# A two-layer hybrid encoder step on one core: when GpSimd adds up layer 1's weight sums in HBM

## The chip, the core and the metric

The kernel runs on one core of a Trainium2 chip. The time is device microseconds of one execution, the median of several runs. The profile is one further execution, recorded by the hardware profiler.

## What is computed

One step of a streaming encoder with two layers over 576 tokens: 512 of a prompt and 64 of a later chunk that attends to 512 cached positions. All arithmetic is float32.

```
h = rmsnorm(x, g_pre_mix);  z = h @ w_in
y_a = b_g * causal_depthwise_conv3(c_g * xin)
y_b = multi-head latent attention (8 heads, rotary key, chunk-causal mask)
x = x + rmsnorm((sigmoid(ga) * y_a + sigmoid(gb) * y_b) @ w_o, g_post_mix)
f = square(relu(rmsnorm(x, g_pre_ffn) @ w1)) @ w2      # 1024 -> 4096 -> 1024
x = x + rmsnorm(f, g_post_ffn)
```

## The kernel before

Features lie on the partitions and tokens on the free axis, in two halves of 288 tokens. Each float32 product is made of three float32r matmuls (mm3, L811 to L813) from a high and a low part of weight and input; ACT copies the high part of a weight block (w_hi), DVE subtracts it from the raw block (w_lo, L2071). The five engines run programs written out by hand, each in order, and meet only through semaphores.

A layer goes through the latent projections (P1), eight heads, the output projection w_o with the later chunk's attention between its blocks, and the feed-forward in eight groups of 512 hidden features (GROUPS). SyncE loads the weights into nine slots as 512 KB blocks (slot_load, L859) or as halves of 256 KB.

Where both token halves are multiplied by the same two-by-two blocks of a weight, the kernel makes seven block products in place of eight, in Strassen's manner (Winograd's form). That needs sums and differences of weight quarters. There are two places:

- Heads 2 to 6 (MIXED of them, two pairs of blocks each). Their weight sums don't depend on data, and GpSimd makes them in HBM, in the tensor weight_sums, by DMAs: one copy of a block's first half into two places and two further copies (sums_copy, L1129 to L1131), then four DMAs that add to what they write (L1135, L1136, L1139, L1142). A sum is four quarters; there are N_SUMS = 20, ten a layer. sums_steps(n0, n1) issues them in a software pipeline: round n copies for sum n + 1, adds first to n, second to n - 1 and third to n - 2, each after the semaphore of what it builds on. SyncE loads finished sums from HBM (L949 and L954) behind a wait on sums_third.
- Feed-forward groups 2 to 7. There DVE makes the sums in SBUF (pair_sums, L3009 to L3014) once both blocks of a couple have landed. A couple, pair(g, p) in the code, is half of a group: seven products into the four PSUM banks named ring (r_pair(g, p, i) numbers them). After the couple come eight products with w2 into the four banks named att (w2_blocks); DVE adds them to my (w2_out, L2923), which frees the bank for the product four later.

In group 3 and later, DVE's order after a couple's last ring product is fixed: the next couple's four pair_sums, one low part of f, the first w2_out, and so on (outs_and_lo). SyncE issues the next couple's first block (pair_load(g, p, 0)) after this couple's second product and the second block after its fifth. ACT takes the first block's high part (block_hi, L1845) before the couple's second output.

GpSimd's program is short: the sums, the rotation of the key in both layers (key_rope, L1175 to L1184) and part of the last addition (L1198). It issues the first two rounds of sums before layer 0's key rotation (BEFORE_KEYS = 2) and all the others right after it, in one sequence over both layers' sums. In head 7 SyncE also loads the caches for the later chunk (L995 to L999), which ACT and DVE split (L1556, L1557, L1567) before they go on with that head's convolution and gates. The last head's merged rows (xs_hi, L1661; xs_lo, L2744) are what w_o needs first.

Of the kernel before, what the change touches and what calls it, by code (L numbers as in the profile page):

```python
# [53 lines left out]
def n_head(h, i):  # L54
    return N_P1 + N_HEAD * h + i
# [30 lines left out]
MIXED = LAST_MIXED - FIRST_MIXED + 1  # L86
# [83 lines left out]
N_SUMS = DEPTH * 2 * MIXED  # L170
BEFORE_KEYS = 2
# [26 lines left out]
def pair_no(L, g, p):  # L198
    return L * PAIRS + 2 * (g - FIRST_PAIR) + p
# [32 lines left out]
def r_pair(g, p, i):  # L232
    return R5 + 7 * pair_no(0, g, p) + i
# [103 lines left out]
def root(L, name):  # L337
    return len(ROOTS) * L + ROOTS.index(name) + 1
# [380 lines left out]
def full(L, idx):  # L719
    return L * RING + (idx + 1)  # L720
# [78 lines left out]
def cols(s):  # L799
    return slice(NH * s, NH * (s + 1))  # L800
# [313 lines left out]
def rotation_and_sums(nc, block, pl, blocks):  # L1114


    @block.gpsimd
    def _(pool):

        def first_and_second(n):  # L1120

            L, i = divmod(n, 2 * MIXED)
            row = n_head(FIRST_MIXED + i // 2, (2, 0)[i % 2])
            return blocks[L * NB + row], blocks[L * NB + row + 1]

        def sums_copy(n):
            a, b = first_and_second(n)
            a11 = a[:, 0:512].unsqueeze(1).broadcast_to([P, 2, 512])
            pool.dma_start(pl.sums[n][:, 0:2, :], a11).then_inc(pl.sums_copied, 16)  # L1129
            pool.dma_start(pl.sums[n][:, 2, :], b[:, 0:512]).then_inc(pl.sums_copied, 16)  # L1130
            pool.dma_start(pl.sums[n][:, 3, :], a[:, 512:1024]).then_inc(pl.sums_copied, 16)  # L1131

        def sums_add_first(n):
            _, b = first_and_second(n)
            pool.dma_start(pl.sums[n][:, 2, :], b[:, 512:1024], accum_op=ALU.add).then_inc(pl.sums_first, 16)  # L1135
            pool.dma_start(pl.sums[n][:, 1, :], b[:, 0:512], accum_op=ALU.add).then_inc(pl.sums_first, 16)  # L1136

        def sums_add_second(n):
            pool.dma_start(pl.sums[n][:, 0, :], pl.sums[n][:, 2, :], accum_op=ALU.add).then_inc(pl.sums_second, 16)  # L1139

        def sums_add_third(n):
            pool.dma_start(pl.sums[n][:, 3, :], pl.sums[n][:, 0, :], accum_op=ALU.add).then_inc(pl.sums_third, 16)  # L1142

        def sums_steps(n0, n1):

            for n in range(n0, n1):
                if n < N_SUMS:
                    pool.wait_ge(pl.sums_copied, 48 * (n + 1))
                if 1 <= n <= N_SUMS:
                    pool.wait_ge(pl.sums_first, 32 * n)  # L1150
                if 2 <= n <= N_SUMS + 1:
                    pool.wait_ge(pl.sums_second, 16 * (n - 1))
                if n >= 3:
                    pool.wait_ge(pl.sums_third, 16 * (n - 2))
                if n + 1 < N_SUMS:
                    sums_copy(n + 1)
                if n < N_SUMS:
                    sums_add_first(n)
                if 1 <= n <= N_SUMS:
                    sums_add_second(n - 1)  # L1160
                if n >= 2:
                    sums_add_third(n - 2)

        pool.sem_inc(pl.ring_free, 4)
        pool.sem_inc(pl.w2_free, 4)
        pool.sem_inc(pl.summed, 2)
        pool.sem_inc(pl.pv_read, 1)

        def key_rope(L, half):

            cs, n = cols(half), 2 * L + half
            pool.wait_ge(pl.key_swapped, n + 1)
            if half == 1:
                pool.wait_ge(pl.key_roped, n)
            nc.gpsimd.tensor_tensor(pl.rope1_t[:, :], pl.kpe[:, cs], pl.cos[:, cs], ALU.mult) \  # L1175
                .then_inc(pl.key_turned, 1)
            nc.gpsimd.tensor_tensor(pl.rope1_s[:, half, :], pl.rope1_s[:, half, :], pl.sin[:, cs], ALU.mult) \
                .then_inc(pl.key_turned, 1)
            pool.wait_ge(pl.key_turned, 3 * n + 2)
            nc.gpsimd.tensor_tensor(pl.rope1_t[:, :], pl.rope1_t[:, :], pl.rope1_s[:, half, :], ALU.add) \  # L1180
                .then_inc(pl.key_turned, 1)
            pool.wait_ge(pl.key_turned, 3 * n + 3)
            pool.wait_ge(pl.rooted, root(L, ("rx_a", "rx_b")[half]))
            nc.gpsimd.tensor_tensor(pl.kpe[:, cs], pl.rope1_t[:, :], pl.rx[:, cs], ALU.mult) \  # L1184
                .then_inc(pl.key_roped, 1)

        pool.wait_ge(pl.x_landed[7], 16)
        sums_copy(0)
        sums_steps(0, BEFORE_KEYS)
        for L in range(DEPTH):  # L1190
            pool.wait_ge(pl.tables_landed, L * 32 + 32)
            key_rope(L, 0)
            key_rope(L, 1)
            if L == 0:
                sums_steps(BEFORE_KEYS, N_SUMS + 2)
        for i, (m0, m1) in enumerate(TAIL_MOVED):
            pool.wait_ge(pl.tail_factored, i + 1)
            nc.gpsimd.tensor_tensor(pl.x[:, m0:m1, cols(1)], pl.x[:, m0:m1, cols(1)], pl.last[:, m0:m1, :], ALU.add) \  # L1198
                .then_inc(pl.tail_moved, 1)
# [2782 lines left out]
```

## Time and profile before

| what | value |
|---|---|
| median of 3 runs | 1727.48 us (1726.52 to 1728.12) |
| the profiled execution's own time | 1726.3 us |
| its span | 1724.5 us |
| mean granted TensorE clock | 0.997 |
| TensorE busy | 1705.7 us, 99% |
| VectorE busy | 1309.3 us, 76% |
| ScalarE busy | 855.1 us, 50% |
| GpSimd busy | 122.3 us, 7% |
| HBM read and written | 214.39 MB and 57.02 MB |

The span runs from the first to the last instruction. PE is TensorE, DVE VectorE, ACT ScalarE, POOL GpSimd and SP SyncE; a q behind a name is the engine's instruction queue. Numbers with L are lines of the kernel. Layer 1 runs the same instructions as layer 0 some 850 us later, so that a moment of one layer can be compared with the other's. The time to landing of a DMA runs from its issue to its semaphore.

### The profile page before, as it was taken

How to read it: one execution, taken by the hardware profiler on the slowest of the kernel's cores; microseconds unless marked ns; L12 is line 12 of the kernel's file. 1: busy time of each engine (PE TensorE's matmuls, PEld its weight loads, DVE VectorE, ACT ScalarE, POOL GpSimd, SP SyncE). 2: the span in 40 equal slices, each digit the busy share in tenths (PEclk: the TensorE clock that was granted, in tenths of full speed). 3: DMA queues.
4: the chain of work that ended last, by engine and by line, in shares of the span. 5: the costliest groups of instructions: out<-in, count | busy, mean ns of one | idle time of the engine just before them, and what ended most of it. 6: DMA issues, size and time to landing. Idle time of an engine off the chain costs nothing.

```text
span 1724.5 us, 31894 instructions
## 1 busy us (share of the span) xinstructions
PE 1705.7 (99%) x12735; PEld 1690.9 (98%) x12735; DVE 1309.3 (76%) x2514; ACT 855.1 (50%) x1665; POOL 122.3 (7%) x163
## 2 busy tenths in 40 slices
PE   9999999999999999999999999999999999999997
PEld 9998999999999999999999999999999999999997
DVE  7788787767798786668687797777678887777665
ACT  7625454545465454436366364545435536444452
POOL 1412121212210000000001000000000000000000
PEclk9999999999999999999999999999999999999998
DMA  7899898898762232323124454343532213322231
GB/s 239 198 212 244 214 209 211 178 249 235 163 129 97 89 96 86 99 86 111 60 84 149 148 166 139 114 121 112 171 117 98 99 37 111 98 86 87 74 99 55
DMA packets 90996, 231.54 MB, mean 134 GB/s; under 512 B 9824, under 2 KB 25440, under 8 KB 90848
## 3 DMA queue, kind: packets, MB, share of 16 engines
q1 hardware_dynamic: 71968, 185.45, 33.5%
q0 software_dynamic: 17600, 41.95, 13.8%
q8 instruction: 101, 1.65, 0.4%
q10 hardware_dynamic: 1280, 2.10, 0.3%
q14 instruction: 47, 0.39, 0.1%
HBM read 214.39 MB, written 57.02 MB: 157 GB/s over the span
## 4 chain that ended last, share of the span: by engine, by line
PE 94%; DMA 2%; DVE 2%; ACT 1%; SPq 1%; issue 0%; DVEq 0%; ACTq 0%
PE ring L811 19%; PE ring L813 19%; PE ring L812 19%; PE att L811 11%; PE att L813 11%; PE att L812 11%; PE att L3527 1%; DMA cache_pe_raw<-cache_pe_in 1%; PE att L806 1%; PE att L805 1%; DMA small_raw<-small_in 1%; DMA xs_lo_raw<-h_kept 1%; PE att L818 0%; ACT rope_s L1291 0%; PE att L3343 0%
## 5 line engine op out<-in xcount | busy, mean ns | idle before, releaser
L811 PE MATMUL ring<-xs_hi,w_lo 128*128 128x288 f32 x1872 | 556.6, 297 | 4.3 <-DVE xs_lo L2744 2.2
L813 PE MATMUL ring<-xs_hi,w_hi 128*128 128x288 f32 x1872 | 551.4, 295 | 0.0
L812 PE MATMUL ring<-xs_lo,w_hi 128*128 128x288 f32 x1872 | 551.3, 294 | 0.0
L2071 DVE TENSOR_TENSOR w_lo<-w_raw,w_hi 128x1024 fp32r<-128x1024 f32 (+1 forms) x364 | 370.0, 1035 | 37.3 <-ACT w_hi L1220 27.2
L811 PEld LDWEIGHTS ring<-xs_hi,w_lo 128*128 128x128 f32 x1872 | 351.6, 188 | 7.3 <-DVE ga L2355 2.4
L812 PEld LDWEIGHTS ring<-xs_lo,w_hi 128*128 128x128 f32 x1872 | 351.7, 188 | 1.4
L813 PEld LDWEIGHTS ring<-xs_hi,w_hi 128*128 128x128 f32 x1872 | 351.5, 188 | 0.0
L813 PE MATMUL att<-f_hi,w_hi 128*128 128x288 f32 x960 | 283.2, 295 | 0.0
L812 PE MATMUL att<-f_lo,w_hi 128*128 128x288 f32 x960 | 282.9, 295 | 0.0
L811 PE MATMUL att<-f_hi,w_lo 128*128 128x288 f32 x960 | 282.6, 294 | 0.0
L811 PEld LDWEIGHTS att<-f_hi,w_lo 128*128 128x128 f32 x960 | 180.4, 188 | 0.0
L812 PEld LDWEIGHTS att<-f_lo,w_hi 128*128 128x128 f32 x960 | 180.4, 188 | 0.0
L813 PEld LDWEIGHTS att<-f_hi,w_hi 128*128 128x128 f32 x960 | 180.4, 188 | 0.0
L1212 ACT ACTIVATE w_hi<-w_raw 128x1024 fp32r<-128x1024 f32 x98 | 101.9, 1053 | 87.0 <-DMA w_raw<-blocks_in 86.8
L1220 ACT ACTIVATE w_hi<-w_raw 128x1024 fp32r<-128x1024 f32 x118 | 122.8, 1051 | 7.2 <-DMA w_raw<-blocks_in 6.5
L2923 DVE TENSOR_TENSOR my<-att,my 128x288 f32<-128x288 f32 x160 | 70.8, 451 | 67.7 <-PE att L813 67.7
L813 PE MATMUL ring<-mix_hi,w_hi 128*128 128x288 f32 x384 | 113.5, 295 | 0.0
L811 PE MATMUL ring<-mix_hi,w_lo 128*128 128x288 f32 x384 | 113.1, 295 | 0.0
L812 PE MATMUL ring<-mix_lo,w_hi 128*128 128x288 f32 x360 | 105.9, 294 | 0.0
L811 PE MATMUL ring<-turn_hi,w_lo 128*128 128x288 f32 x320 | 94.9, 296 | 0.0
L812 PE MATMUL ring<-turn_lo,w_hi 128*128 128x288 f32 x320 | 94.4, 295 | 0.0
L813 PE MATMUL ring<-turn_hi,w_hi 128*128 128x288 f32 x320 | 94.2, 295 | 0.0
(342 smaller groups left out, 3184.4 us busy)
## 6 DMA issues: line engine op xcount, KB each, us to landing
w_raw<-blocks_in SPq DMA_DIRECT2D x195, 512.0 KB, 3.7
weight_sums<-blocks_in POOLq DMA_DIRECT2D x80, 256.0 KB, 7.2
w_raw<-blocks_in SPq DMA_DIRECT2D x62, 256.0 KB, 4.6
weight_sums<-blocks_in POOLq DMA_DIRECT2D x20, 512.0 KB, 5.6
weight_sums<-weight_sums POOLq DMA_DIRECT2D x40, 256.0 KB, 7.6
w_raw<-weight_sums SPq DMA_DIRECT2D x20, 512.0 KB, 4.6
w_raw<-weight_sums SPq DMA_DIRECT2D x40, 256.0 KB, 4.4
small_raw<-small_in SPq DMA_DIRECT2D x16, 320.0 KB, 4.6
```

The lines of the kernel that those rows point to most:

```text
L805: pe.matmul(out, both, keys[1], start=False, stop=False)
L806: return pe.matmul(out, both, keys[0], start=False, stop=True)
L811: pe.matmul(out, w[1], x[0], start=first, stop=False)
L812: pe.matmul(out, w[0], x[1], start=False, stop=False)
L813: return pe.matmul(out, w[0], x[0], start=False, stop=last)
L1212: act.activation(hi, raw, ACT.Copy).then_inc(pl.weights_hi, 1)
L1220: act.activation(hi, raw, ACT.Copy).then_inc(pl.weights_hi, 1)
L2071: return dve.tensor_tensor(out, a, hi.bitcast(F32), ALU.subtract)
L2923: dve.tensor_tensor(dst, src, dst, ALU.add).then_inc(pl.w2_free, 1)
L3527: last = pe.transpose(att[:, to:to + P], pl.probs[:, PO[t] + P * j:PO[t] + P * (j + 1)], ident)
```

## The change

sums_steps takes two further arguments, the first sum and the end of the stretch that its pipeline runs over. GpSimd now runs it over layer 0's ten sums alone, to the end (2 * MIXED = 10), waits until the last is done and until the ring product r_pair(2, 1, 0) of layer 0 is full, and then runs it over layer 1's ten. r_pair(2, 1, 0) is the first product of the second couple of feed-forward group 2. The other engines' programs are as before.

```diff
--- before.py
+++ after.py
@@ -1141,24 +1141,24 @@
         def sums_add_third(n):
             pool.dma_start(pl.sums[n][:, 3, :], pl.sums[n][:, 0, :], accum_op=ALU.add).then_inc(pl.sums_third, 16)
 
-        def sums_steps(n0, n1):
+        def sums_steps(n0, n1, first, end):
 
             for n in range(n0, n1):
-                if n < N_SUMS:
+                if n < end:
                     pool.wait_ge(pl.sums_copied, 48 * (n + 1))
-                if 1 <= n <= N_SUMS:
+                if first < n <= end:
                     pool.wait_ge(pl.sums_first, 32 * n)
-                if 2 <= n <= N_SUMS + 1:
+                if first + 1 < n <= end + 1:
                     pool.wait_ge(pl.sums_second, 16 * (n - 1))
-                if n >= 3:
+                if n > first + 2:
                     pool.wait_ge(pl.sums_third, 16 * (n - 2))
-                if n + 1 < N_SUMS:
+                if n + 1 < end:
                     sums_copy(n + 1)
-                if n < N_SUMS:
+                if n < end:
                     sums_add_first(n)
-                if 1 <= n <= N_SUMS:
+                if first < n <= end:
                     sums_add_second(n - 1)
-                if n >= 2:
+                if n > first + 1:
                     sums_add_third(n - 2)
 
         pool.sem_inc(pl.ring_free, 4)
@@ -1186,13 +1186,17 @@
 
         pool.wait_ge(pl.x_landed[7], 16)
         sums_copy(0)
-        sums_steps(0, BEFORE_KEYS)
+        sums_steps(0, BEFORE_KEYS, 0, 2 * MIXED)
         for L in range(DEPTH):
             pool.wait_ge(pl.tables_landed, L * 32 + 32)
             key_rope(L, 0)
             key_rope(L, 1)
             if L == 0:
-                sums_steps(BEFORE_KEYS, N_SUMS + 2)
+                sums_steps(BEFORE_KEYS, 2 * MIXED + 2, 0, 2 * MIXED)
+                pool.wait_ge(pl.sums_third, 16 * 2 * MIXED)
+                pool.wait_ge(pl.ring_full, full(0, r_pair(2, 1, 0)))
+                sums_copy(2 * MIXED)
+                sums_steps(2 * MIXED, N_SUMS + 2, 2 * MIXED, N_SUMS)
         for i, (m0, m1) in enumerate(TAIL_MOVED):
             pool.wait_ge(pl.tail_factored, i + 1)
             nc.gpsimd.tensor_tensor(pl.x[:, m0:m1, cols(1)], pl.x[:, m0:m1, cols(1)], pl.last[:, m0:m1, :], ALU.add) \
```

GpSimd's instructions, in order, behind layer 0's key rotation, from the round that copies for the eleventh sum (layer 1's first). Before:

```order
L1129 DMA weight_sums<-blocks_in 128x2x512 [waits sums_second,sums_third,sums_first,sums_copied]
L1130 DMA weight_sums<-blocks_in 128x512
L1131 DMA weight_sums<-blocks_in 128x512
L1135 DMA weight_sums<-blocks_in 128x512
L1136 DMA weight_sums<-blocks_in 128x512
L1139 DMA weight_sums<-weight_sums 128x512
L1142 DMA weight_sums<-weight_sums 128x512
```

The same place with the change:

```order
L1135 DMA weight_sums<-blocks_in 128x512 [waits sums_second,sums_third,sums_first,sums_copied]
L1136 DMA weight_sums<-blocks_in 128x512
L1139 DMA weight_sums<-weight_sums 128x512
L1142 DMA weight_sums<-weight_sums 128x512
L1139 DMA weight_sums<-weight_sums 128x512 [waits sums_third,sums_second,sums_first]
L1142 DMA weight_sums<-weight_sums 128x512
L1142 DMA weight_sums<-weight_sums 128x512 [waits sums_third,sums_second]
L1129 DMA weight_sums<-blocks_in 128x2x512 [waits ring_full,sums_third]
L1130 DMA weight_sums<-blocks_in 128x512
L1131 DMA weight_sums<-blocks_in 128x512
L1129 DMA weight_sums<-blocks_in 128x2x512 [waits sums_copied]
L1130 DMA weight_sums<-blocks_in 128x512
```

The round's three copies are gone from there, the pipeline drains over three rounds, and the copies for layer 1's first sum stand behind a wait on ring_full; from there the ten sums follow each other as the first ten did.

## Rows read from the trace of the kernel before

**Rows 1.** The page: TensorE's busy time, and the chain that ended last, by engine

```profile
PE 1705.7 (99%) x12735; PEld 1690.9 (98%) x12735; DVE 1309.3 (76%) x2514; ACT 855.1 (50%) x1665; POOL 122.3 (7%) x163
...
PE 94%; DMA 2%; DVE 2%; ACT 1%; SPq 1%; issue 0%; DVEq 0%; ACTq 0%
```

**Rows 2.** Timeline of PE: start, duration (us), instruction, idle time before and its releaser

```profile
136.47 0.50 PE L811 MATMUL att<-probs_t_hi,v_lo 128*128 128x512 f32 x1 [2.44 <-DVE probs_t_lo L2071]
...
402.92 0.37 PE L811 MATMUL ring<-xs_hi,w_lo 128*128 128x288 f32 x1 [2.21 <-DVE xs_lo L2744]
```

**Rows 3.** Table by stage; the first row names its columns

```profile
core 0: us, PE busy (x) PEld busy (x) DVE busy (x) ACT busy (x) POOL busy (x), PEclk, DMA share, GB/s
160.00:372.00 212.00, 212.00 (x1565) 208.77 (x1564) 165.04 (x334) 102.59 (x191) 44.38 (x60) 1.00 0.86 207
372.00:410.00 38.00, 35.79 (x267) 35.22 (x267) 27.73 (x63) 20.03 (x45) 6.88 (x9) 1.00 0.96 239
457.00:510.00 53.00, 53.00 (x402) 53.00 (x401) 51.67 (x107) 33.49 (x73) 11.01 (x14) 1.00 0.70 155
591.00:791.00 200.00, 200.00 (x1512) 200.00 (x1511) 143.03 (x266) 94.92 (x187) 0.00 (x0) 1.00 0.30 90
1008.00:1222.00 214.00, 213.65 (x1576) 210.34 (x1576) 167.00 (x336) 104.63 (x196) 0.00 (x0) 1.00 0.42 127
1222.00:1258.00 36.00, 36.00 (x270) 35.65 (x269) 27.46 (x61) 19.22 (x43) 0.00 (x0) 1.00 0.48 150
```

**Rows 4.** Issues of the sums (first and last start, us); timeline of PE, second couple

```profile
L1129 POOL DMA_DIRECT2D weight_sums<-blocks_in x20: 724/751/885, 19.2 to 458.8; - x20
...
L949 SPq DMA_DIRECT2D w_raw<-weight_sums x20: 319/323/339, 116.6 to 1183.5; - x20
...
589.14 0.29 PE L811 MATMUL ring<-xs_hi,w_lo 128*128 128x288 f32 x1
```

**Rows 5.** Timeline of SP, ACT and DVE around head 7's cache loads, in both layers

```profile
375.67 0.43 SPq L981 DMA_DIRECT2D small_raw<-small_in  x1
...
1226.57 0.43 SPq L981 DMA_DIRECT2D small_raw<-small_in  x1
...
390.78 1.06 ACT L1556 ACTIVATE cache_t_hi<-cache_t_raw 128x1024 fp32r<-128x1024 f32 x1 [1.99 <-DMA cache_pe_raw<-cache_pe_in]
...
402.32 0.45 DVE L2744 SCALAR_TENSOR_TENSOR xs_lo<-my,xs_hi 128x288 fp32r<-128x288 f32 x1
...
1250.11 0.45 DVE L2744 SCALAR_TENSOR_TENSOR xs_lo<-my,xs_hi 128x288 fp32r<-128x288 f32 x1
```

**Rows 6.** Timeline of PE and DVE at a couple's end in layer 0's feed-forward

```profile
706.78 0.29 PE L811 MATMUL att<-f_hi,w_lo 128*128 128x288 f32 x1
...
719.50 0.29 PE L811 MATMUL ring<-xs_hi,w_lo 128*128 128x288 f32 x1
...
707.40 0.69 DVE L3009 TENSOR_TENSOR w_raw<-w_raw 128x512 f32<-128x512 f32 x1
...
710.31 0.45 DVE L2923 TENSOR_TENSOR my<-att,my 128x288 f32<-128x288 f32 x1
```

**Rows 7.** DMA issues, median us to landing: 160:372 (two), 1008:1222 (two), 591:791 (one)

```profile
w_raw<-blocks_in SPq DMA_DIRECT2D x10, 512.0 KB, 7.9
w_raw<-weight_sums SPq DMA_DIRECT2D x9, 512.0 KB, 5.7
...
w_raw<-blocks_in SPq DMA_DIRECT2D x10, 512.0 KB, 3.5
w_raw<-weight_sums SPq DMA_DIRECT2D x9, 512.0 KB, 3.8
...
w_raw<-blocks_in SPq DMA_DIRECT2D x34, 512.0 KB, 3.5
```

**Rows 8.** The page's queues: packets, MB, time as a share of 16 engines' span

```profile
q1 hardware_dynamic: 71968, 185.45, 33.5%
q0 software_dynamic: 17600, 41.95, 13.8%
```

## The prediction, as made before the change was run

> **What bounds the kernel now.** The page first: TensorE is busy 1705.7 us of a span of 1724.5 us, and 94% of the chain that ended last is its own work [rows 1]. So a change pays only where TensorE stands still, and costs only where it makes TensorE stand still. TensorE's waits come next, and where they lie in time: the two longest are 2.44 us at 136.47 us, for the probabilities' low parts, and 2.21 us at 402.92 us, for xs_lo of L2744 [rows 2]. The first lies while layer 0's own sums are under way, which the change leaves as they are. The table by stage then shows that of layer 0's stages from 160 us on TensorE is idle in one alone, 372 to 410 us (35.79 of 38.00 us busy), and that the DMA engines are 0.86 busy in the heads (160 to 372 us) and 0.96 there, against 0.42 and 0.48 in the same stages of layer 1, where no sums are made; in the feed-forward they are 0.30 busy [rows 3]. The granted clock is 1.00 in every one of these rows, so it plays no part.
>
> **What the change moves.** Nothing is removed. Twenty sums are issued by GpSimd, from 19.2 us on, the last one's copy at 458.8 us [rows 4]: one per 23.1 us, and two further rounds end the last, at some 505 us. The first ten (layer 0's) keep their place. The other ten, layer 1's, now wait until the first product of group 2's second couple is full. That couple's products begin at 589.14 us [rows 4] and a product takes 1.59 us (below), so the wait ends at 590.7 us. Behind it on GpSimd stand only the sums themselves and, after them, layer 1's key rotation. SyncE waits for sums before it loads them, in layer 0 first at 116.6 us [rows 4]; layer 1 runs 850.90 us behind (below), so its first such load is due at 967.5 us. With 20 to 23 us each the ten sums end at 790 to 820 us: nobody is late for them, this costs nothing, and the cover is some 150 us. Two extra bursts on GpSimd's queue (the tail of the first ten, the start of the second ten) cost nothing either, GpSimd being idle there. What is left is the traffic: it goes out of some 300 to 505 us and comes into 591 to about 810 us.
>
> **The gain, at 402.9 us.** Head 7 loads its small block, the cache and weight blocks close together. The small block's issue on SyncE at 375.67 us has its twin in layer 1 at 1226.57 us, 850.90 us later. ACT stands idle 1.99 us for cache_pe in layer 0; at the end of the chain DVE's xs_lo starts at 402.32 us, where the twin (1250.11 less 850.90) would start at 399.21 us: 3.11 us late, of which TensorE waits 2.21 us [rows 5]. The twin makes TensorE wait for nothing. The instructions are the same; what differs is the sums' traffic. The whole 2.21 us should go. Bounds: nothing (if the load order alone made it) and 2.21 us; I take 2.2, since the twin is the nearest row there is. What is late next there has 0.9 us in hand (3.11 less 2.21).
>
> **The loss, from 591 us on.** Here the reader must look at how narrow a couple's schedule is. TensorE makes seven ring products and then eight att products; the latter begin at 706.78 us and the next couple at 719.50 us, that is 1.59 us a product, and 15 of them or 23.85 us a couple. The fifth att product starts halfway, at 713.14 us, and needs its bank emptied by DVE's first L2923, which ends at 710.31 + 0.45 = 710.76 us: 2.4 us in hand [rows 6]. In front of it on DVE, which works in order, stand the four weight sums L3009 to L3014. The first starts at 707.40 us, when the couple's second weight block lands (it lands 3.5 us after its issue, the median of all 34 loads of the stretch [rows 7]; the issue follows TensorE's fifth product at 719.50 − 23.85 + 5 × 1.59 = 703.6 us, so the two agree), and DVE works without a pause from there to L2923. So a block that lands d late makes TensorE wait d − 2.4 us, once per couple. The couple's first block holds ACT in the same way, but was issued three products earlier; I leave it out.
>
> How late does a load land beside the sums? The trace has it for the heads, with equal loads in both layers. Ten 512 KB loads from blocks_in land in 7.9 us (median) in 160 to 372 us and in 3.5 us in layer 1: d = 4.4. Nine loads from weight_sums: 5.7 against 3.8 us, d = 1.9 [rows 7]. Over the slack of 2.4 that is 2.0 us for ten and nothing for nine: 20/19 = 1.05 us a load. The feed-forward loads less itself (DMA share 0.30 against 0.42 [rows 3]), so less queues behind a late load: 1.05 × 0.30/0.42 = 0.75 us. The sums last 200 to 230 us, that is nine couples: 9 × 0.75 = **6.7 us**. Bounds: nothing, if every d stays under 2.4 (the nine), and 9 × 2.0 = 18 us if every load is as late as the median of the ten.
>
> What speaks against this loss is the size of a load in engine time. The rows on the queues [rows 8]: SyncE's queue holds 16 engines for 33.5% of 1724.5 us for 185.45 MB, so 1.63 us for a 512 KB load; GpSimd's 13.8% is 238 us, 11.9 us a sum, half of the time in which sums are made. If the engines took turns evenly, a load of 1.63 us would be held up by about as much again, 1.6 us, less than the slack; the ten loads at d = 4.4 say that it is more. The Trainium skill, DMA: Bandwidth & Descriptors, section Queues, rings and completion order, states such turns: each DMA engine goes round the queues that have work, a whole packet at a time. By that rule the loss would be nought and the change would give 2.2 us. By the rows the loss is 6.7 us, and I go by them; even turns stay a rival.
>
> **Sum.** 1726.3 us is the profiled execution's time, 1.2 us under the median of the runs (1727.48). 1726.3 − 2.2 + 6.7 = 1730.8; on the median's footing 1727.5 + 4.5 = **1732.0 us**.
>
> **Rivals.** (1) The slack holds: the sums find the DMA engines 70% idle, their turns are even, d stays under 2.4 us, and only the 2.2 us at 402.9 us remain: 1725.3 us, not slower. For it: 457 to 510 us, with sums and weight loads at once, shows no wait of TensorE (53.00 us of 53.00 busy [rows 3]). Against it: the medians of rows 7 (the loads of 457 to 510 us may have more time before their use). It decides at d = 2.4 us. (2) The sums fall into step with the couples (20 to 23 us against 23.85 us) and hit the sensitive load nearly every time: 9 × 2.0 = 18 us, 1743 us. Against it: the two cadences differ by 1 to 4 us, so over nine couples they drift through each other. (3) The couples' loads get by, and the wait at 136.47 us shrinks as well: 1727.5 − 2.2 − 2.4 = 1722.9 us. Nothing in the trace ties that wait to layer 1's sums. (4) The wait passes at once and nothing moves: excluded by the value it waits for, which the ring reaches first at 590.7 us.
>
> **Chances.** What a measurement of this kernel can tell from no change is 0.2%, 3.5 us. The forecast has 0.53: its own spread is a loss of 4 to 11 us, net +2 to +9, and a quarter of it (0.13) stays within 3.5 us. Rival 1 has 0.33, rival 2 0.08, rival 3 0.06. So slower 0.40 + 0.08 = 0.48, same 0.13 + 0.33 = 0.46, faster 0.06. The predicted time is the forecast's. The range goes down to rival 1 with a little room, 1724.5, and up to a net +11, 1738.5, short of rival 2. The forecast's own range is 1729.5 to 1736.5.
>
> **What would show it.** In the changed kernel's trace: GpSimd's copies stop near 250 us and start again at about 591 us; DMA share near 0.45 to 0.5 in 372 to 510 us and 0.7 or more in 591 to 800 us; the wait for xs_lo L2744 gone from TensorE's list; w_raw's landing time in 591 to 791 us at 5 us or more; and new TensorE waits for my of L2923, each 0.5 to 2.5 us, at the fifth att product of a couple. The forecast is wrong if those waits are missing or add up to less than 3 us, if the landing times stay under 5.9 us, or if the wait at 402.9 us stays.

## The result, and the profile after

The changed kernel takes 1730.27 us (median of 13 runs, 1726.34 to 1732.39) against 1725.07 us for the kernel before on the same chips (13 runs, 1723.38 to 1728.12). The ratio is 1.0023, with a 95% interval from 1.0014 to 1.0032: 4.0 us slower, 2.4 to 5.5 (the ratio is formed over runs side by side, so it isn't that of the two medians). Its profiled execution has a span of 1730.6 us, 6.1 us above that of before, and its own time, 1732.39 us, is the longest of the 13.

TensorE's list of waits in the changed kernel (us in total, times, longest). L2927 is L2923 of before, L2075 is L2071; the change put four lines ahead of them:

```profile
PE att L811 <- DVE my L2927: 6.3, 5, 2.5
PE att L811 <- DVE probs_t_lo L2075: 2.1, 1, 2.1
```

The wait for xs_lo of L2744, 2.21 us before [rows 2], is no longer in the list; five waits for my take its place. The wait for probs_t_lo is still there (2.1 us against 2.4). Where the five lie, from the timeline of TensorE (start, duration, idle time before it):

```profile
615.94 0.40 PE L811 MATMUL att<-xs_hi,w_lo 128*128 128x288 f32 x1 [0.63 <-DVE my L2927]
...
640.57 0.40 PE L811 MATMUL att<-xs_hi,w_lo 128*128 128x288 f32 x1 [0.50 <-DVE my L2927]
...
738.02 0.40 PE L811 MATMUL att<-f_hi,w_lo 128*128 128x288 f32 x1 [1.53 <-DVE my L2927]
...
763.27 0.40 PE L811 MATMUL att<-f_hi,w_lo 128*128 128x288 f32 x1 [1.14 <-DVE my L2927]
...
789.83 0.40 PE L811 MATMUL att<-f_hi,w_lo 128*128 128x288 f32 x1 [2.46 <-DVE my L2927]
```

The table by stage of the changed kernel, to be held against [rows 3] (the same columns):

```profile
372.00:410.00 38.00, 38.00 (x286) 37.65 (x285) 29.50 (x68) 19.91 (x46) 0.00 (x0) 1.00 0.52 174
457.00:510.00 53.00, 53.00 (x402) 53.00 (x402) 50.30 (x104) 33.51 (x75) 0.00 (x0) 1.00 0.24 80
591.00:791.00 200.00, 193.74 (x1453) 192.33 (x1452) 134.55 (x252) 93.74 (x182) 46.17 (x63) 1.00 0.82 186
```

TensorE is now fully busy at head 7 and idle 6.3 us in the feed-forward. The DMA share fell from 0.96 to 0.52 at head 7 and from 0.70 to 0.24 in 457 to 510 us, and rose from 0.30 to 0.82 in 591 to 791 us: the traffic went where the prediction put it. GpSimd's wait ended at 589.0 us and the weight loads beside the sums land in 6.0 us in place of 3.5 [rows 7], 2.5 us late:

```profile
589.00 0.75 POOL L1129 DMA_DIRECT2D weight_sums<-blocks_in  x1 [331.72 <-PE ring L813]
...
w_raw<-blocks_in SPq DMA_DIRECT2D x33, 512.0 KB, 6.0
```

The sums' last DMA landed at 817.6 us. All eight couples of the loop over groups 3 to 6 lie beside them, and five of the eight have a wait.

The longest of the five waits in full. The load, issued at 777.85 us as the couple's second block, takes 8.5 us and lands at 786.3 us; DVE stands 4.04 us (the profile names no releaser, but goes on 0.1 us after this landing) and starts L3013 (L3009 of before) at 786.41 us; its first L2927 starts 2.91 us later, as in [rows 6], and TensorE stands until 789.83 us (the DMA issue, then DVE's timeline):

```profile
w_raw<-blocks_in SPq DMA_DIRECT2D x1, 512.0 KB, 8.5
...
786.41 0.69 DVE L3013 TENSOR_TENSOR w_raw<-w_raw 128x512 f32<-128x512 f32 x1 [4.04 <-issue]
...
789.32 0.45 DVE L2927 TENSOR_TENSOR my<-att,my 128x288 f32<-128x288 f32 x1
```

d is 8.5 − 3.5 = 5.0 us and the wait 2.46, so the slack was 2.5; the prediction had worked out 2.4. The waits at 640.57 and 738.02 us came in the same way, with second blocks 3.0 and 4.0 us late.

The other two came by another path. At 763.27 us the couple's first block was late: issued at 747.8 us, it took 9.0 us. ACT, which copies its high part before it goes on with f, stood 6.28 us for it, and DVE stood 3.96 us for ACT before it could reach its four sums (the issue, then the timelines of ACT and DVE):

```profile
w_raw<-blocks_in SPq DMA_DIRECT2D x1, 512.0 KB, 9.0
...
756.82 1.06 ACT L1849 ACTIVATE w_hi<-w_raw 128x1024 fp32r<-128x1024 f32 x1 [6.28 <-DMA w_raw<-blocks_in]
...
759.12 0.46 DVE L2075 TENSOR_TENSOR f_lo<-ff,f_hi 128x288 fp32r<-128x288 f32 x1 [3.96 <-ACT f_hi L1826]
```

The second block of that couple landed at 758.9 us, before DVE had come that far (759.86 us). At 615.94 us it was the same: the first block took 7.3 us, the second only 4.0. So 4.5 us of the 6.3 came from second blocks and 1.8 us from first blocks.

**The balance.** Three moments of TensorE's work divide the run: layer 0's first product with turn_hi, its first with mix_hi and its last with mix_hi. In the kernel before (timeline of TensorE):

```profile
159.49 0.30 PE L811 MATMUL ring<-turn_hi,w_lo 128*128 128x288 f32 x1
...
568.47 0.29 PE L811 MATMUL ring<-mix_hi,w_lo 128*128 128x288 f32 x1
...
811.60 0.30 PE L813 MATMUL ring<-mix_hi,w_hi 128*128 128x288 f32 x1
```

and in the changed kernel:

```profile
159.38 0.29 PE L811 MATMUL ring<-turn_hi,w_lo 128*128 128x288 f32 x1
...
565.86 0.29 PE L811 MATMUL ring<-mix_hi,w_lo 128*128 128x288 f32 x1
...
818.31 0.30 PE L813 MATMUL ring<-mix_hi,w_hi 128*128 128x288 f32 x1
```

The first stretch went from 408.98 to 406.48 us: a gain of 2.5. The second went from 243.13 to 252.45 us: a loss of 9.3. The waits give 6.3 of it. Another 1.6 us is the clock. The table in steps of 2 us shows the granted clock fall behind the wait of 2.46 us to its lower level, 1.2 GHz (0.50). It stayed there for 3.41 us. The timeline has the matmuls 0.24 us apart in this stretch and 0.13 us apart after it, which makes the 1.6 us:

```profile
790.00:792.00 2.00, 2.00 (x14) 2.00 (x15) 2.00 (x6) 1.17 (x2) 1.72 (x3) 0.84 0.68 76
792.00:794.00 2.00, 2.00 (x11) 2.00 (x9) 2.00 (x4) 0.00 (x0) 0.00 (x0) 0.50 0.89 64
794.00:796.00 2.00, 2.00 (x14) 2.00 (x14) 2.00 (x5) 0.00 (x0) 0.00 (x0) 0.80 1.02 178
796.00:798.00 2.00, 2.00 (x17) 2.00 (x17) 0.56 (x2) 0.00 (x0) 0.01 (x1) 1.00 0.43 77
```

Two of the matmuls at the lower level, from the timeline:

```profile
792.32 0.44 PE L811 MATMUL att<-f_hi,w_lo 128*128 128x288 f32 x1
792.56 0.44 PE L812 MATMUL att<-f_lo,w_hi 128*128 128x288 f32 x1
```

Another 1.3 us is 0.26 us at each of the five waits, beyond the idle time shown: a couple with a wait of 1.14 us took 25.25 us in place of 23.85. Of the 0.26 us, 0.16 lie in front of the wait: the profile counts a matmul as busy past the moment at which the next could have started (0.29 us long at a spacing of 0.13 us), so a gap looks shorter than it is. The other 0.10 lie behind it: the second matmul after the wait starts 0.23 us after the first. The last 0.2 us is a hitch at 664 us, too short for the list.

### The profile page after: what moved, and what is told of

It reads as the page before. It is cut to its first block, busy times and chain, and to the rows that moved or that the text cites. A ratio compares the mean times of both kernels' runs of the same rounds, so it can differ in the third digit from the quotient of the medians.

```text
span 1730.6 us, 31893 instructions
## 1 busy us (share of the span) xinstructions
PE 1708.4 (99%) x12735; PEld 1692.6 (98%) x12735; DVE 1311.4 (76%) x2514; ACT 855.3 (49%) x1665; POOL 122.4 (7%) x163
## 4 chain that ended last, share of the span: by engine, by line
PE 92%; DMA 3%; DVE 2%; issue 1%; ACT 1%; SPq 0%; DVEq 0%
PE ring L811 19%; PE ring L813 19%; PE ring L812 19%; PE att L811 11%; PE att L813 10%; PE att L812 10%; DMA w_raw<-blocks_in 2%; PE att L3531 1%; DMA xs_lo_raw<-h_kept 1%; PE att L806 1%; PE att L805 1%; DMA small_raw<-small_in 1%; PE att L818 0%; PE att L3347 0%; PE att L819 0%
## 5 line engine op out<-in xcount | busy, mean ns | idle before, releaser
L2075 DVE TENSOR_TENSOR w_lo<-w_raw,w_hi 128x1024 fp32r<-128x1024 f32 (+1 forms) x364 | 370.9, 1038 | 45.5 <-ACT w_hi L1224 26.6
L2927 DVE TENSOR_TENSOR my<-att,my 128x288 f32<-128x288 f32 x160 | 70.5, 452 | 53.8 <-PE att L813 53.6
```

Source lines behind the costliest of these rows:

```text
L2075: return dve.tensor_tensor(out, a, hi.bitcast(F32), ALU.subtract)
L2927: dve.tensor_tensor(dst, src, dst, ALU.add).then_inc(pl.w2_free, 1)
```

## The experiments

Theory: a DMA of the sums that is ahead of a weight load in the DMA engines makes it late by d; where d is more than 2.4 us for a couple's second block, TensorE stands for the rest. Rivals: other causes in the feed-forward, the clock, or a gain that isn't the sums'. All ratios below are against the kernel before, run beside them on the same chip.

### The gain alone

```diff
 def head_sums(L, h, c):
-    return 2 * MIXED * L + 2 * (h - FIRST_MIXED) + c
+    return 2 * (h - FIRST_MIXED) + c
...
                 sums_steps(BEFORE_KEYS, 2 * MIXED + 2, 0, 2 * MIXED)
-                pool.wait_ge(pl.sums_third, 16 * 2 * MIXED)
-                pool.wait_ge(pl.ring_full, full(0, r_pair(2, 1, 0)))
-                sums_copy(2 * MIXED)
-                sums_steps(2 * MIXED, N_SUMS + 2, 2 * MIXED, N_SUMS)
```

> Layer 1's ten sums are left out altogether, and layer 1's heads load layer 0's sums in their place, so layer 1's output is not the reference's; the loads are as many and as large. Theory (gain of 2.2 us at head 7, loss only through the feed-forward's loads): the gain stands alone, 2.2 us under the kernel before (ratio 0.9987), no TensorE wait for xs_lo L2744 in layer 0 and none for my of w2_out; against the changed kernel about 6 us less. Rival (the sums' traffic costs time in many small places that TensorE's list does not show): more than 4 us under the kernel before. Rival (the changed kernel's extra time has nothing to do with the sums in the feed-forward): no more than 2 us under the changed kernel.

Measured: ratio 0.9979 (0.9965 to 0.9993), 3.6 us under the kernel before, median 1723.56 against 1726.06 us. TensorE's list has neither xs_lo L2744 nor my; the first stretch took 406.43 us and the second 243.13. So layer 1's sums cost about 2.5 to 3.6 us in their old place, and with the changed kernel's ratio of 1.0023 they cost over 7 us in the new one. Of the 4.1 us by which the two spans differ, 2.5 us lie in the first stretch; the rest lies before 160 us and behind the last product, where both kernels run the same instructions. No place but head 7 shows a saving. The interval reaches from 1.2 to 6.0 us, so that the time alone doesn't exclude many small savings; the stretches speak against them.

### The order on DVE

```diff
             def outs_and_lo(g, k0, g0, p0, g1, p1):
 
+                w2_out(g, k0)
                 pair_sums(g1, p1)
                 f_done(g0, p0, 2)
-                w2_out(g, k0)
                 f_done(g0, p0, 3)
```

> The changed kernel with one instruction of DVE moved: after a couple, the first w2_out goes ahead of the four weight sums, so the fifth att product no longer waits for the block's landing; the second w2_out does, with 3.6 us in hand in place of 2.4. Theory (TensorE waits d minus the slack): the five waits of 0.64, 0.51, 1.54, 1.14 and 2.47 us shrink by 1.2 each, to about 1.6 us in all; the time comes 4 to 6 us under the changed kernel, near or a little under the kernel before (ratio 0.999 to 1.000). Rival (the time is lost in the DMA engines or the clock and DVE's order is no matter): TensorE's waits stay near 6 us, merely under another name, and the time stays at 1.002.

Measured: 1.0006 (0.9991 to 1.0021). TensorE's waits for my, with the sums where the change put them:

```profile
PE att L811 <- DVE probs_t_lo L2075: 3.4, 1, 3.4
PE att L811 <- DVE my L2927: 1.5, 6, 0.4
```

1.5 us in place of 6.3, where 1.6 was expected from the five waits less the wider slack. The second stretch took 247.44 us, so that 4.3 us of the 9.3 are left: 1.5 of these waits, 0.7 of a wait for ft near 810 us and 0.26 us at each of the seven. The time came out 3 us below the changed kernel's ratio rather than the 4 to 6 expected. The intervals are too wide to tell 3 from 4, and what else may be missing isn't shown. (This profile also has 3.4 us of wait for probs_t_lo at 137 us, with a lowered clock behind it, which the edit doesn't touch.) So most of the waiting arises where a late block meets DVE's order; a part of the loss stays with the order changed.

The reorder by itself, on the kernel before:

> The kernel before with only DVE's order changed (the first w2_out ahead of the four weight sums). It shows what the reorder itself costs. Theory: nothing, no wait of TensorE in the feed-forward, ratio 0.9995 to 1.0005. Rival (e3's time above the kernel before came from the reorder): small waits of TensorE in every couple of both layers, ratio 1.001 or above.

Measured: 1.0010 (0.9997 to 1.0023), not to be told from no change. No wait of TensorE in any couple, second stretch 243.13 us: the reorder costs nothing there. But this execution waited longer at head 7, where its program is that of the kernel before:

```profile
404.40 0.58 PE L811 MATMUL ring<-xs_hi,w_lo 128*128 128x288 f32 x1 [4.50 <-DVE xs_lo L2744]
```

So the 2.21 us of [rows 2] is one draw. With the sums in their old place that wait was 2.21, 4.50, 1.64 and 3.00 us in four profiles; the gain of taking them away varies with it.

### A late block without any sums beside it

```diff
-                after_pair(g, 0, 4)
+                after_pair(g, 0, 6)
                 pair_load(g, 1, 1)
...
-                after_pair(g, 1, 4)
+                after_pair(g, 1, 6)
                 pair_load(g + 1, 0, 1)
```

> The kernel before, sums in their old place, but SyncE issues the second block of each of the couples of the loop over groups 3 to 6 after the couple's seventh product in place of the fifth: d = 2 x 1.59 = 3.2 us late without any sums beside it, 8 times a layer. Theory: TensorE waits d - 2.4 = 0.8 us in each of the 16 couples for my of w2_out and loses 0.26 us more in restarting: 17 us slower, ratio 1.010, and the couples' waits all alike. Rival (the slack is wider, and the changed kernel's waits came from elsewhere): no waits, ratio 1.000.

Measured: 1.0093 (1.0064 to 1.0122), 16 us.

```profile
PE att L811 <- DVE my L2923: 12.8, 16, 1.6
```

Sixteen waits, all but one of them between 0.6 and 1.0 us, 12.8 us in all (16 × 0.8 = 12.8). The second stretch and its twin in layer 1 took 251.04 and 252.10 us, 16.9 us more than twice 243.13; that leaves 4.1 us, or 0.26 us a wait, for the restart. This settles the slack of 2.4 us and the price of a late second block, with the sums out of the picture. The largest wait, 1.61 us, lies in layer 1; its block took 4.4 us to land where the others took 3.5 or 3.6.

With the load later still (after w2_filled(L, g - 1, 1) and w2_filled(L, g - 1, 9)):

> As the run with the second block late, but the load goes out after the couple's second att product: d = 4 x 1.59 = 6.4 us. Theory of the wait: TensorE stands 3.9 us in each of the 16 couples and loses 0.26 us more. Theory of the clock: every one of these waits is longer than the shortest that was followed by a lowered clock so far (2.47 us), so each is followed by 3.4 us at 1.2 GHz and costs 1.7 us more: 94 us in all, about 1820 us, with 16 stretches of lowered clock. Rival (the lowered clock is a matter of chance or of the sums' traffic): 67 us in all, about 1793 us, and none or few such stretches.

Measured: one profiled run, 1837.6 us, 111 us above the kernel before.

```profile
PE att L811 <- DVE my L2923: 62.5, 16, 4.1
PE ring L811 <- DVE xs_lo L2744: 3.0, 1, 3.0
PE att L3527 <- DVE probs L2429: 2.9, 1, 2.9
```

The waits are 62.5 us, where 16 × 3.9 = 62.4 was expected. Every one of the sixteen waits had a stretch at 1.2 GHz with it, so the sums are not needed for that; but 14 of the stretches lasted 6.83 us instead of 3.41. The table by 2 us around one of them:

```profile
686.00:688.00 2.00, 0.29 (x1) 0.29 (x2) 1.97 (x6) 1.91 (x4) 0.00 (x0) 0.70 0.33 135
688.00:690.00 2.00, 2.00 (x9) 2.00 (x9) 2.00 (x6) 0.54 (x1) 0.00 (x0) 0.50 0.04 8
690.00:692.00 2.00, 2.00 (x10) 2.00 (x10) 2.00 (x4) 0.00 (x0) 0.00 (x0) 0.50 0.00 0
692.00:694.00 2.00, 2.00 (x11) 2.00 (x11) 1.79 (x5) 0.00 (x0) 0.00 (x0) 0.59 0.00 0
694.00:696.00 2.00, 2.00 (x17) 2.00 (x16) 0.76 (x2) 0.00 (x0) 0.00 (x0) 1.00 0.00 0
```

Part of each longer stretch lies inside the wait itself, as in the first row. Such a couple took 30.70 us, 6.85 over 23.85: 3.9 of wait, 0.26 of restart and 2.7 of clock, where 1.7 was expected. That is most of the 17 us by which the time passed the expected 94; two further waits of 2.9 and 3.0 us at head 7, in this program's old part, make up the rest.

### One sum DMA at a time

The seven DMAs of each of layer 1's sums are issued one after the other; behind each of them stands a wait such as the first one's:

```diff
+            pool.dma_start(pl.sums[n][:, 0:2, :], a11).then_inc(pl.sums_copied, 16)
+            pool.wait_ge(pl.sums_copied, 48 * n + 16)
```

> The changed kernel, but each of layer 1's 70 sum DMAs waits until the one before has landed; the same bytes in some 300 us in place of 220, so at most one is in flight. Theory (a weight load is late by what is queued ahead of it in the DMA engines, up to 5 us with several sum DMAs out, at most 1.5 us for one of 256 KB and 2.9 us for the copy of 512 KB): hardly a load is later than the slack of 2.4 us, the waits for my of w2_out add up to under 1 us, and the time is 2 us under the kernel before. Rival (the sums' accumulating traffic slows HBM for everybody, queued or not): the loads are late as often as the traffic is there, waits of 4 us or more in all, time 1.001 or above.

Measured: 1.0297 (1.027 to 1.0324). The time is a miss, for a reason that the expectation forgot: the ten sums took 376 us, not 300, and layer 1's key rotation stands behind them on GpSimd. It started at 965 us in place of 904 in the kernel before, and TensorE waited for it once. This wait was the longest of all runs; the granted clock was at 1.2 GHz for 58 us, from within it to some 6 us behind it:

```profile
PE att L811 <- DVE rope_t L2411: 55.3, 2, 54.7
PE att L811 <- DVE probs_t_lo L2093: 2.4, 1, 2.4
...
965.11 0.79 POOL L1193 TENSOR_TENSOR rope_t<-kpe,cos 128x288 f32<-128x288 f32 x1 [4.24 <-DMA weight_sums<-weight_sums]
```

The feed-forward of the same run still answers the question. TensorE waits for my nowhere, and the second stretch took 243.13 us; the stage and the loads' landing:

```profile
591.00:791.00 200.00, 200.00 (x1512) 200.00 (x1510) 143.22 (x266) 94.44 (x185) 26.89 (x37) 1.00 0.60 147
...
w_raw<-blocks_in SPq DMA_DIRECT2D x33, 512.0 KB, 4.3
```

The loads are 0.8 us late in place of 2.5. The share of the DMA engines that the sums add fell from 0.52 to 0.30, that is to 58%, the lateness to 32%. So the lateness fell by more than the traffic did. That fits the theory that the number of sum DMAs out at once counts. It doesn't show it: the rate of the traffic was changed together with it, and nothing here says that lateness grows in proportion to traffic.

### The start moved

> The changed kernel with the wait for layer 1's ten sums placed earlier: the first block of w_o (about 408 us) in place of the feed-forward's second couple. The sums then run from 408 to some 640 us. Theory: all of the 2.5 us at head 7 are gained, and only the three or four couples before 640 us are exposed, so that 0 to 3 us are lost: ratio 0.9985 to 1.0003, TensorE waits for my only before 650 us. Rival (sums next to the loads of w_o and of the first two groups cost as much as next to the couples): TensorE waits from 408 to 560 us and a ratio of 1.002.

Measured: 1.0026 (1.0013 to 1.0039); outside what was expected. Its list:

```profile
PE att L811 <- DVE my L2927: 2.9, 1, 2.9
...
PE ring L811 <- issue: 1.8, 2, 1.5
```

One couple was hit, at 621.6 us, for 2.86 us with 3.41 us of lowered clock behind it. That wait came by the first block: it took 9.6 us, ACT stood for it and DVE for ACT, and the second block had landed 2.9 us before DVE came to its sums:

```profile
616.35 0.46 DVE L2075 TENSOR_TENSOR f_lo<-ff,f_hi 128x288 fp32r<-128x288 f32 x1 [4.56 <-ACT f_hi L1826]
```

TensorE also stood 1.46 us at 565.6 us, at the first product of the first couple, group 2's. The profile names no releaser, but the program waits there for the third low part of that couple's weights, which DVE finished 0.1 us before. The couple's second block had taken 7.5 us to land, against 3.5 us in the kernel before. The expectation counted waits in couples from group 3 on; that the sums also reach the loads in front of the first couple was the rival's point, and it holds in part.

> The changed kernel with the wait 13 us later, at the first product of group 3's first couple (about 601 us in place of 588). Theory (which loads are hit depends on how the sums' bursts fall, the number hit on how long they last): again 4 to 7 waits for my of w2_out, other couples than before, 4 to 9 us in all; ratio 1.001 to 1.004. Rival (the sums lock to the couples' rhythm at one phase): either no waits at all or nearly every couple, beyond 12 us.

Measured: 1.0053 (1.0033 to 1.0072), more than expected. Five waits for my, 8.6 us in all:

```profile
PE att L811 <- DVE my L2927: 8.6, 5, 3.2
```

Four of them lie near 641, 669, 696 and 793 us, three in a row; the fifth, near 615 us, is under 0.2 us. The one near 696 us came by a first block of 9.3 us, the other three by second blocks. Neither none nor all of the couples are hit: the sums don't lock to the couples. The waits add up to 8.6 us in place of 6.3, and the ratio went from 1.0023 to 1.0053. With one profile of each start, how much of the difference in waits is the start and how much is scatter isn't shown.

### A pause over head 7

The kernel before with one wait:

```diff
+PAUSE = 14
...
             for n in range(n0, n1):
+                if n == PAUSE:
+                    pool.wait_ge(pl.ring_full, full(0, WO_A[0]))
```

> The kernel before with one wait added: the sums run on through the heads as before, stop before round 14 until the first block of w_o is full (about 408 us) and then go on, to end near 540 us, before the first couple's loads. Theory: only the sums at head 7 cost anything, so the 2.2 us are gained and nothing is lost: ratio 0.9987 (0.998 to 0.9995), TensorE's wait for xs_lo L2744 gone, no wait for my of w2_out. Rival (the sums later, at 510 to 540 us, disturb the loads of the first couples): waits of 1 us or more near 560 to 600 us and no gain.

Measured: 0.9983 (0.9969 to 0.9996), median 1724.71 us against 1726.06. The wait at head 7 is gone; one came back at the first w2 product. Four weight loads issued one behind the other from 508.4 us on took 7.0 to 9.7 us beside the last sums; the same four took 3.5 to 8.0 us in the kernel before, whose sums had ended. So they were 1.6 to 3.5 us late, not the 4 us that the run with the shorter pause, below, was planned with (the timelines of TensorE and DVE):

```profile
524.83 0.37 PE L812 MATMUL att<-f_hi,w_lo 128*128 128x288 f32 x1 [1.14 <-issue]
...
524.28 0.45 DVE L2910 TENSOR_SCALAR rx<-att 128x288 f32<-128x288 f32 x1
```

The profile names no releaser here. The program waits at this place for DVE's L2910 (L2907 of before), which ended 0.1 us earlier and stands in DVE's order behind the low parts of these blocks.

> The paused kernel (resumed at the first block of w_o) once more, beside the shorter pause on the same chip. Theory: ratio 0.9975 to 0.9990 again. Rival (the first result was luck of 5 rounds): its interval includes 1.

Measured: 0.9987 (0.9977 to 0.9997), median 1724.35 against 1726.38 us. The wait near 525 us was 2.99 us this time, again 0.1 us behind the end of L2910.

> The paused kernel, but the sums go on 16 us sooner, when head 7's eighth ring product is full (392 us in place of 408), behind the cache's landing. In the paused kernel four w2 loads issued at 508 to 514 us were 4 us late beside the last sums and TensorE stood 1.14 us at 524.8 us. Theory: that wait shrinks (0 to 0.8 us), nothing comes back at head 7, ratio 0.9975 to 0.999 and up to 1 us under the paused kernel. Rival (the sums from 392 us on still delay head 7's last steps): a wait for xs_lo L2744 of 0.5 us or more near 400 us, ratio 0.999 to 1.000.

(The resumption waits for r_hd(HEADS - 1, 3, 1) in place of WO_A[0].) Measured: 0.9993 (0.9981 to 1.0004). In its profile both the wait at head 7 and the one near 525 us are gone, as the theory has it, and its span is 1722.0 us, but over its runs it can't be told from the kernel before nor from the longer pause. The paused kernel beats the kernel before in two sets of runs, by 2 to 3 us, and by its ratio it lies 6 to 7 us under the changed one.

## Why the prediction was right, and where its sizes were off

- **The two places** were right. TensorE loses its wait at head 7 and gets new ones at the fifth att product, between 0.5 and 2.5 us, in five couples. The prediction counted nine couples beside the sums; eight have the order on which its slack rests.
- **The gain** was put at 2.2 us and came to 2.5: the wait of 2.21 and 0.29 us of restart that the prediction did not count. That the twin in layer 1 names the cause is borne out by the run without the second ten sums. The wait, which the prediction took for a fixed number, is a draw between 1.6 and 4.5 us.
- **The slack** of 2.4 us was right for the second block: the late block alone gave 16 waits of 0.8 us at d = 3.2, and 3.9 us at d = 6.4.
- **The first block** was left out of the prediction as issued three products earlier. That was wrong for loads as late as these. Two of the five waits, 1.8 of 6.3 us, came by a first block, through ACT: it was 5.5 us late at 763.27 us and 3.1 us late at 615.94 us (7.3 against 4.2 us for the same load in the kernel before). With the start moved to 408 us the one wait in a couple, 2.86 us, came by it too. No run makes a first block late by itself, so its slack isn't measured on its own.
- **The lateness** was put at 0.75 us beyond the slack a load, 6.7 us over nine; the waits came to 6.3. That the two are so near is luck in part. The second blocks, for which alone the sum was made, gave 4.5 us, and the first blocks made up for the difference. Of the eight second blocks three were 3.0 us or more late and made waits, one was 2.8 us late in a couple that waited for its first block, and four were 2.4 us late or less. The scaling by DMA share was a guess that no run tests; a start 13 us later gave 8.6.
- **Missing terms**: 0.26 us of restart at each wait (1.3 us) and the clock behind the longest wait (1.6 us). They make the loss 9.3 us in the profiled execution, where 6.7 was forecast. Over the runs the net is 4.0 us, where 4.5 was forecast. This too is luck in part: the profiled execution, in which the terms can be counted, is 6.1 us slower than that of before and the slowest of its 13. The others must have lost less, and no trace shows where.
- **The cover** of some 150 us was reckoned to layer 1's first load of a sum. Layer 1's key rotation, behind the sums on GpSimd, is due sooner, at 904 us in the kernel before. With the sums ended at 817.6 us the cover was some 86 us, enough here; the run with one DMA at a time overran it.
- **The rivals.** That the slack holds (rival 1) is refuted: loads were up to 5.6 us late (9.1 us to landing) with 1.63 us of own work. The Trainium skill (DMA: Bandwidth & Descriptors, Queues, rings and completion order) has each DMA engine go round the queues with work, a whole packet at a time. From such turns, taken as even, the prediction estimated about 1.6 us of delay. The rows of 8.5 and 9.0 us refute that estimate of a load's delay; whether the turns themselves are even, no run here shows. No lock-step was seen, and no saving at 136 us beyond the scatter of that wait (2.44 us before, 2.09 us after).
- **What stays open**: how much of a load's lateness is the number of sum DMAs out and how much their traffic; how far the waits of one start differ from execution to execution, since the changed kernel has one profile.

## What to carry to other kernels

Background DMAs are paid for where a load has the least slack: before such traffic is moved into a stage with idle DMA engines, find every load whose landing the in-order engines wait for, and how long until TensorE notices; a load left out because it is issued early can still be the one that decides. A twin stage of the same kernel, with and without the traffic, gives an estimate of the price and of how many loads are late. Here a short pause over the one narrow place gained 2 to 3 us where the move lost 4, and one bank drained ahead of the waiting instruction cut the waits in the couples from 6.3 to 1.5 us.

## What the runs showed of the hardware

- A wait of TensorE costs about 0.26 us more than its idle time shows, at a matmul spacing of 0.13 us: in the kernel with the late second block, 16 waits of 12.8 us in all made the two stretches in which they lie 16.9 us longer (251.04 and 252.10 us against 243.13 each).
- The granted clock fell to 1.2 GHz, during the wait or up to 1.6 us behind it, with waits of TensorE of 2.46 (twice), 2.80, 2.86, 2.93, 2.99, 3.00, 3.22, 3.40 and 4.50 us and all sixteen of 3.8 to 4.1 us. It stayed there for 3.41 us, or for 6.83 us in 14 of the sixteen, and for 58 us over the wait of 54.7 us. Between TensorE's first and last long products it did not fall with waits of 2.44, 2.42, 2.37, 2.22, 2.21 us and shorter ones. With it, the wait of 2.46 us in the changed kernel cost 2.46 + 0.26 + 1.6 = 4.3 us.
- A 512 KB load, 1.63 us of engine time by the page, landed in 6.0 us (median of 33) and up to 9.1 us beside the sums' DMAs from GpSimd's queue, against 3.5 us (median of 34) without them.
